# Issuing ten small parameter transfers from ScalarE's queue instead of SyncE's

## The reference, cut to what matters

```python
silu_c = jax.nn.silu(c)
silu_cc = jax.nn.silu(c_ctx)[None]
x_lat, x_ctx = x, ctx
for i in range(DEPTH):
    mod_l = jnp.split((silu_c @ ada_w[i] + ada_b[i])[:, None], 6, axis=-1)
    mod_c = jnp.split((silu_cc @ ada_w[i] + ada_b[i])[:, None], 6, axis=-1)
    ...
    h_lat = rmsnorm(x_lat, norm_w[i, 0]) * (1 + sc_l) + sh_l
    h_ctx = rmsnorm(x_ctx, norm_w[i, 0]) * (1 + sc_c) + sh_c
    ...
return rmsnorm(x_lat, final_norm_w)
```

## Time and profile before

| quantity | value |
|---|---|
| median of 3 runs | 2173.82 us (2170.48 to 2175.4) |
| time of the profiled execution | 2175.86 us |
| span of the profiled execution | 2174.1 us |
| PE busy | 2097.9 us, 96% of the span |
| DVE busy | 1085.4 us, 50% |
| ACT busy | 825.7 us, 38% |
| POOL busy | 49.7 us, 2% |
| mean DMA rate | 94 GB/s |

### The profile page before, as it was taken

The page is one execution under the profiler, slowest core; times in us unless marked ns, Lnnn a source line. Parts: engine busy times, 40 slices in busy tenths (PEclk is TensorE's granted clock), DMA queues, the critical chain, the costliest instruction groups (busy, mean ns, idle before and its releaser), DMA issues.

```text
span 2174.1 us, 33801 instructions
## 1 busy us (share of the span) xinstructions
PE 2097.9 (96%) x13385; PEld 1873.6 (86%) x13400; DVE 1085.4 (50%) x1600; ACT 825.7 (38%) x1283; POOL 49.7 (2%) x78
## 2 busy tenths in 40 slices
PE   6999999999999999999999999999998999999998
PEld 4899999998989999999999887777775788888887
DVE  6655555557462222222233687787777644333334
ACT  3544433434232221122221563838383425522222
POOL 1000000000000000000000100000001000000000
PEclk8999999999999999999999899999999999999999
DMA  7422222213323332233321221121215232332331
GB/s 274 156 88 61 86 79 88 88 60 117 116 90 113 112 99 67 77 113 114 114 80 46 88 62 46 46 81 47 87 48 211 70 97 77 96 106 87 96 109 66
DMA packets 297512, 204.42 MB, mean 94 GB/s; under 512 B 5012, under 2 KB 289037, under 8 KB 295629
## 3 DMA queue, kind: packets, MB, share of 16 engines
q1 hardware_dynamic: 293965, 180.03, 27.4%
q0 software_dynamic: 3456, 23.09, 2.7%
HBM read 189.47 MB, written 13.63 MB: 93 GB/s over the span
## 4 chain that ended last, share of the span: by engine, by line
PE 83%; DVE 8%; ACT 5%; issue 2%; DMA 1%; SPq 0%; ACTq 0%; POOL 0%; DVEq 0%
PE G L312 70%; PE G L421 2%; ACT e L1419 1%; PE S L775 1%; PE S L1544 1%; DVE acc L1575 1%; PE S L746 1%; PE S L1540 1%; DVE wlo L299 1%; ACT whi L295 1%; DVE hn L647 1%; DVE hlo L656 1%; DMA adalo<-in_ada_w_dram 1%; PE G L427 1%; PE S L1746 1%
## 5 line engine op out<-in xcount | busy, mean ns | idle before, releaser
L312 PE MATMUL G<-hhi,whi 128*128 128x384 f32 (+2 forms) x2336 | 726.6, 369 | 27.6 <-DVE hlo L656 17.7
L312 PE MATMUL G<-hhi,wlo 128*128 128x384 f32 (+2 forms) x2336 | 680.5, 349 | 0.0
L312 PE MATMUL G<-hlo,whi 128*128 128x384 f32 (+2 forms) x2336 | 680.1, 349 | 0.0
L299 DVE TENSOR_TENSOR wlo<-raw,whi 128x1024 fp32r<-128x1024 f32 (+1 forms) x225 | 288.0, 1280 | 762.1 <-ACT whi L295 761.8
L295 ACT ACTIVATE whi<-raw 128x1024 fp32r<-128x1024 f32 (+1 forms) x225 | 249.1, 1107 | 946.0 <-PE G L312 469.6
L312 PEld LDWEIGHTS G<-hhi,whi 128*128 128x128 f32 x2336 | 422.4, 191 | 93.7 <-issue 39.1
L312 PEld LDWEIGHTS G<-hhi,wlo 128*128 128x128 f32 x2336 | 432.9, 190 | 20.2
L312 PEld LDWEIGHTS G<-hlo,whi 128*128 128x128 f32 x2336 | 433.2, 190 | 17.3
L312 PE MATMUL G<-mhi,whi 128*128 128x384 f32 (+2 forms) x550 | 165.6, 346 | 0.0
L312 PE MATMUL G<-mhi,wlo 128*128 128x384 f32 (+2 forms) x550 | 165.2, 345 | 0.0
L312 PE MATMUL G<-mlo,whi 128*128 128x384 f32 (+2 forms) x550 | 165.2, 345 | 0.0
(11 more groups left out here) (287 smaller groups left out, 2074.1 us busy)
## 6 DMA issues: line engine op xcount, KB each, us to landing
raw<-in_ffn_w_in_dram SPq DMA_DIRECT2D x88, 512.0 KB, 3.7
raw<-in_ffn_w_out_dram SPq DMA_DIRECT2D x32, 704.0 KB, 4.5
raw<-in_ssm_w_in_dram SPq DMA_DIRECT2D x41, 512.0 KB, 3.8
raw<-in_hg_w_in_dram SPq DMA_DIRECT2D x40, 512.0 KB, 3.7
adaw<-in_ada_w_dram SPq DMA_DIRECT2D x20, 1024.0 KB, 5.4
adaf<-in_ada_w_dram SPq DMA_DIRECT2D x20, 1024.0 KB, 5.0
raw<-in_ssm_w_out_dram SPq DMA_DIRECT2D x16, 512.0 KB, 3.9
ada<-in_ada_w_dram SPq DMA_DIRECT2D x2, 2048.0 KB, 13.0
```

The lines of the kernel that those rows point to most:

```text
L299: dve.tensor_tensor(wlo[pn.slot][:, 0:kt, :], raw[pn.slot][:, 0:kt, :], f32(whi[pn.slot][:, 0:kt, :]), ALU.subtract).then_inc(s["lo"], 1)
L312: ins = pe.matmul(G[:, tl.slot, g0:g0 + n], w[pn.slot][:, k, :], r[:, k_base + k, t0:t0 + n], start=(first and k == 0 and i == 0), stop=(l ...
```

## The change

The block that describes the ten small transfers and the loop that issues them move, unchanged, from the head of SyncE's program to the head of ScalarE's, ahead of its first wait. Their sources, targets, order and semaphore stay. Nothing else changes.

```diff
         @block_.sync
         def _(sp):
-            rows = ((m["rowA"], COL_NORM, norm_w.rearrange("l i (j p) -> (l i j) p", p=P)),
-                    (m["rowA"], COL_FIN, final_norm_w.rearrange("(j p) -> j p", p=P)),
...
-                    (m["rowD"], 0, hg_lb.rearrange("d r (h p) -> (d r h) p", p=P)))
-            for to, r0, src in rows:
-                sp.dma_start(to[r0:r0 + src.shape[0], :], src).then_inc(s["rows"], 16)
             for b in range(NBLK):
                 src = x[0] if b < LBLK else ctx_x[0]
                 b0 = b if b < LBLK else b - LBLK
...
         @block_.scalar
         def _(act):
+            rows = ((m["rowA"], COL_NORM, norm_w.rearrange("l i (j p) -> (l i j) p", p=P)),
+                    (m["rowA"], COL_FIN, final_norm_w.rearrange("(j p) -> j p", p=P)),
...
+                    (m["rowD"], 0, hg_lb.rearrange("d r (h p) -> (d r h) p", p=P)))
+            for to, r0, src in rows:
+                act.dma_start(to[r0:r0 + src.shape[0], :], src).then_inc(s["rows"], 16)
             act.wait_ge(s["cols"], 1)
```

More of the change, by code:

```diff
@@ L2057, in _ @@
         def _(act):
+            rows = ((m["rowA"], COL_NORM, norm_w.rearrange("l i (j p) -> (l i j) p", p=P)),
+                    (m["rowA"], COL_FIN, final_norm_w.rearrange("(j p) -> j p", p=P)),
+                    (m["rowA"], COL_C, c.rearrange("b (j p) -> (b j) p", p=P)),
+                    (m["rowA"], COL_CC, c_ctx.rearrange("(j p) -> j p", p=P)),
+                    (m["rowA"], COL_SN, ssm_norm_w.rearrange("b (j p) -> (b j) p", p=P)),
+                    (m["rowA"], COL_CB, ssm_conv_b.rearrange("b (j p) -> (b j) p", p=P)),
+                    (m["rowA"], COL_GN, hg_norm_w),
+                    (m["rowB"], 0, ada_b.rearrange("l (t p) -> (l t) p", p=P)),
+                    (m["rowC"], 0, ssm_conv_w.rearrange("b k (t p) -> (b k t) p", p=P)),
+                    (m["rowD"], 0, hg_lb.rearrange("d r (h p) -> (d r h) p", p=P)))
+            for to, r0, src in rows:
+                act.dma_start(to[r0:r0 + src.shape[0], :], src).then_inc(s["rows"], 16)
             act.wait_ge(s["cols"], 1)
```

## The result

The changed kernel has a median of 2180.7 us (2176.04 to 2183.18, 20 runs), the kernel before 2174.89 us (2170.48 to 2178.62, 20 runs). The ratio is 1.0023, with a 95% interval from 1.0017 to 1.0029: slower by 0.23%, or 5 us; the two medians differ by 5.8 us. The forecast was 2174.3 us with a range to 2178.8, so the time lies outside it. About 1.1 us of the miss is the baseline: the forecast started from the median of three runs of the kernel before, 2173.82 us, and twenty give 2174.89. With that added the range would end at 2179.9, and the time still lies outside.

The account below looks back on a forecast made before the run. Bounded by two start chains: adalo about 3.3 us earlier, but late rows delay VectorE 1.5 us, using up its 1.02 us slack. First product and end move +0.5 us: median 2174.3 us, range 2170.0 to 2178.8.

Parts of the forecast that it names:

- What bounds the start: Start of the program, up to the first matrix product: SyncE's ten issues take 3.86 us, the ceiling of the saving.
- The two chains: At the start: SyncE's issues, adalo and TensorE; and parameter rows, TensorE, VectorE; 1.02 us apart at 28 to 29 us.
- ScalarE's issues at no cost: Head of ScalarE: ten issues end at 4.64, the table load at 5.9, before the columns arrive; both cost nothing.
- Rival B: ScalarE's last row issues get stuck behind SyncE's; rows complete at 16.2, time 2181.2 us, slower; chance 0.09.
- The rows into the crowd: Row transfers beside xin's packets on the DMA engines: complete between 7.6 and 10.0 us, taken as 9.3.
- The turn by turn price: On the DMA engines a small packet waits for a large one each time: 0.13 to 0.20 us a turn, 36 turns.
- the dear end: Row landing with strictly alternating packets on the DMA engines: 0.20 us a turn, 7.2 us in all, complete at 10.0.
- The queue begins when xin's data begin, at about 2.2: Row transfers on the DMA engines: their 36 turns, 4.8 to 7.2 us, were counted from about 2.2 us.
- The sentence on packets already accepted: Row landing: an issued transfer also stands behind packets the engines have accepted; a reason to take 9.3, nearer 10.0.
- Rival C: Engines serve all of a transfer's packets before turning queues; rows complete at 15.2, time 2180.2 us; chance 0.06.
- Rival D: TensorE, after waiting for VectorE, turns strips and spreads factors at half clock: up to 2 to 3 us, 2177; chance 0.11.
- Same against slower: Whole kernel's outcome: within 0.2% of before, chance 0.79; slower by over 0.2%, 0.15.

## Why the prediction was wrong, by its steps

**What bounds the start.** Right in the main. The two chains were the right frame: the saved 3.86 us did reach SyncE's queue, adalo stopped being the limit, and everything hung on VectorE's start. That they lie 1.02 us apart holds for the one profile that was read; in the second profile of before there is no such wait, and VectorE's chain ends last already. The link from the rows to the strip copy was right in size: the sum has the second strip copy 20.3 us behind the rows (9.3 to 29.6), and the changed kernel shows 12.26 to about 32.4, 20.1 us.

**ScalarE's issues at no cost.** Nearly right: they ended at 5.3 instead of 4.64, the table load moved to 5.33, before it was needed. Rival B's stall did not come. But rowD was issued at 4.80 and not at 4.25, and this 0.55 us stands in the landing; with no tokens beside the rows it was 4.41.

**The rows into the crowd.** This is the first term that was mis-sized. The landing was priced at 7.6 to 10.0, taken as 9.3, and measured at 12.26, 3.0 us more than taken and outside its own bounds. The turn by turn price was right: the last three transfers have 20 turns, and 0.19 us a turn was measured where the dear end had 0.20. The failed step is "The queue begins when xin's data begin, at about 2.2". It lets all 36 turns run from there. But the last three transfers are issued from 3.88 on, and their first packet is served 4.0 us later: 3.88 + 4.0 + 3.9 = 11.8, and the last landing follows at 12.13. The sentence on packets already accepted named the lag, but it only served to choose within the bounds instead of being added. The end of the range of a transfer that comes last must start from its own issue.

**Rival C and the skill.** "DMA: Bandwidth & Descriptors", section "Queues, rings and completion order", of the Trainium skill, has an engine drain a packet of some 9 to 17 descriptors before it turns. By it the rows would have been complete at 15.2. The trace disagrees: behind nearly each of 256 row packets comes a packet of the tokens, and the order with the large ones first served 310 packets of ScalarE's queue against 345 of SyncE's in 3.5 us. The turns are short, as forecast; the measurement decides. The counts of the earlier trace rows alone could not tell it, since turns of some ten packets on either side would give the same shares. The page's rule and the result lie on the same side of the forecast, but the landing was late by the lag and not by long turns.

**Rival D.** The second failed step. The clock was put as a case beside the forecast, with a chance of 0.11 and "up to 2 to 3 us". It was no other case: as soon as VectorE's chain is the last, TensorE waits before the turning, here 4.98 us, and the half clock follows in each of three profiles. Measured, it is 2.2 us from the start of the turning to the first product: 1.6 us on the turning, and 0.5 of the 0.8 on the spreading. The sum should have held it.

**The account.** 0.5 forecast + 3.0 rows + 2.2 clock = 5.7, against 5.6 us at the first product and 5.7 between the profile of before that the forecast used (2175.86) and the one of the larger group after (2181.55). Against the second profile of before (2174.69) the first product is 7.0 us later and the end 6.9, so about 1.4 us of the account depends on which execution of before is taken. That the clock's 2.2 us reach the median is not shown (2180.3 with the pause filled).

**Same against slower.** The chance of 0.15 for slower was too low. Its ways were rivals B and C, stalls and long turns that did not come, and the upper edge of rival D; the late rows and the clock together, two plain terms, were not among them.

## What to carry to other kernels

Before small transfers are moved to a second queue beside bulk ones, ask what waits for the last of them: here each paid a lag and then a turn per packet, so the wait for all of them ended later than it did in front of the bulk. Large ones first is the cheaper order (rows used at 10.07 instead of 12.26). If that wait heads an engine's program, first move the use of the small data behind work that only needs the bulk; with that done, here, the same change brought the first product 4.6 us forward, with 2 to 4 us at the end that the intervals don't secure. And a new wait ahead of TensorE's small work is to be priced with the half clock in the sum, not as a rival.

## What the runs showed of the hardware

A one-row transfer of 512 B beside 4 KB packets took 4.56 us to land, against 1.87 us for 48 rows alone. Small packets got their turns one for one only behind this lag: 107 in 3.5 us in one order of issue, 310 in another, beside 339 and 345 packets of SyncE's queue. Halving the size of the neighbours' packets left the lag near 4 us (3.6), cut the turn from 0.19 to 0.12 us and brought the same ten transfers to use at 10.47 instead of 12.26.

Filling a pause of TensorE kept its clock up through the turning in both profiles that had it, saved 2.1 to 2.2 us at the first product, and still left the median where it was (2180.3 against 2180.7). Two executions of one kernel with starts alike to 0.13 us ended 4.2 us apart. Whether a gain at the start is given back by later changes of the clock is not settled by these runs: it would take profiles of many executions of each kernel.
